# A two-layer decoder block on one core: squares on ScalarE, first units in pairs, norms read one unit later, another order in the layer opening

## The chip, the core and the metric

The kernel runs on one core of a Trainium2 chip. The metric is the device time of one launch in microseconds (us). The five engines are TensorE (PE in the rows, PEld is its weight load), VectorE (DVE), ScalarE (ACT), GpSimd (POOL) and SyncE (SP), which here only issues loads. Each runs its own instruction stream in order and waits on semaphores. A "q" behind a name (SPq, ACTq) is the engine's sequencer, which issues its DMAs.

## The reference, cut to what matters

```python
for l in range(2):
    z = rms_norm(x, mix_norm[l]) @ w_in[l]                 # x: 512 tokens x 1024
    c_q, c_kv, k_r, hq, hf, hi, hg, guv, gates = split(z)
    y_a = mla(...) @ w_branch_a[l]                         # latent attention, 8 heads
    y_b = hgrn2(hq, hf, hi, hg, lower_bounds[l], ...) @ w_branch_b[l]
    y_c = gmlp(guv, gm_ln_g[l], gm_ln_b[l], gm_w_s[l], gm_b_s[l]) @ w_branch_c[l]
    x = x + (g_a * y_a + g_b * y_b + g_c * y_c) @ w_mix_out[l]
    x = x + cross_attn(rms_norm(x, xa_norm[l]), rms_norm(mem, mem_norm[l]), ...)
    gt, up = split(rms_norm(x, ffn_norm[l]) @ ffn_w_in[l])
    x = x + (silu(gt) * up) @ ffn_w_out[l]
return rms_norm(x, final_norm)
```

gmlp takes gelu of u and v, a layer norm of v, a matmul over tokens and u times the result. hgrn2 is a gated linear recurrence in 4 heads; before its products it needs the logarithm of a forget gate made from hf.

## The kernel before, in words

x is kept transposed in SBUF: `xT` has 8 k-tiles of 128 features by 512 tokens. Matmuls run in a split form: each operand is a high part (rounded to fp32r) and a low part (the rest), and one k-tile of a product is three matmuls (high x high, high x low, low x high). hH and hL are the two parts of x times the norm's gain. The rms factor is not in them; it is applied when a product leaves PSUM, by a multiplication with `rh` on VectorE (line 1301).

The work is cut into **units**, one per 128 output columns: 24 matmuls over 8 k-tiles for those from h. A unit's weights go through three engines: SyncE loads them into one of 3 `raw` slots, ScalarE copies them to the high part in one of 4 `wH` slots (`split`, line 936), GpSimd subtracts for the low part (line 513, called a product of GpSimd below: 128x1024). A raw slot is free when GpSimd is done with it, a wH slot when TensorE has finished the unit four places earlier. The first loads of a layer wait for a count of GpSimd that also counts what GpSimd does before the layers.

`plan()` writes the order by hand: units (`u("gv", 0)`) and other steps between them. TensorE walks PLAN. ScalarE and VectorE walk READERS_PLAN, which differs in that ("norm", "mix") and ("norm", "ffn") stand one entry earlier. A step means something on each engine. The steps that matter below:

- `("norm", which)`: TensorE multiplies `sqs`, the sum of squares of x, with ones (line 660), ScalarE takes the root into rh (947), VectorE its reciprocal (1348). No unit from h can leave PSUM before.
- `gv`, `gu`: the two halves of the gMLP; scaled by rh, then gelu on ScalarE (975). `gm_sum`, `gm_mean`, `gm_var`: the layer norm of gv: gm_mean's matmul, centring, squares on ScalarE (1075), their sum on VectorE (1433), gm_var's matmul (674), root (1079), reciprocal (1437), scaling and gain (1440, 1443). `gm_vt` transposes gv on TensorE and ScalarE copies it to gvt (1083); `gm_mix` multiplies (688) and VectorE works on the result (1450, 1454, 1306).
- `lb`: some 25 tiny VectorE operations with three visits to ScalarE, for the lower bounds of the forget gate. `f_1`, `f_2`, `f_3` make the gate's logarithm. `angle` steps are four VectorE operations each on 32x512 for the rotary angles (angle_op).
- `hg_lf`: transposes the logarithm; ScalarE and VectorE split it (1097, 1306). `hg_exp` is the first product of the recurrence (713).
- `xk`, `xv`, `xq`, `x_s`: keys, values, queries and scores of the cross attention. `mix`, `xo`, `fo` end in the residual: VectorE adds to xT (1284), ScalarE makes hH and the square (902, 906), VectorE makes hL and adds the square to sqs (1264, 1274).

Before the layers, TensorE transposes x, ScalarE copies each k-tile from PSUM to xT (912) and makes hH, GpSimd squares (503), and VectorE makes hL and adds the square. k-tile 7 is left to the start of the loop over layers, where ScalarE makes four splits and then its hH and square. 7 PSUM banks are handed out in turn; the 8th is kept for long sums.

## Time and profile before

| | |
|---|---|
| time, median of 3 runs | 2306.24 us (2301.65 to 2307.18) |
| span of the profiled execution, first to last instruction | 2302.0 us |
| TensorE busy | 2206.0 us (96%) |
| VectorE, ScalarE, GpSimd busy | 54%, 43%, 39% |
| mean granted clock of TensorE | 0.990 of full |

Of the profiled execution only the span is recorded; it is 4.2 us below the median of the runs and inside their spread. In the rows a timeline line is: start in us, duration in us, engine, line of the kernel, operation, output<-inputs, count, and in brackets the engine's idle time before it and who ended it. A line of waits is: engine, waiting line <- awaited line: us in total, times, longest. Granted clock 1.00 is TensorE's 2.4 GHz, 0.50 its 1.2 GHz.

### The profile page before, as it was taken

The page shows a single profiled execution, that of the slowest core. Times are in us where ns is not written, and L with a number is a line of the kernel's source. Part 1 is how long each engine was busy: PE and PEld are TensorE (multiplying, and loading weights), DVE is VectorE, ACT ScalarE, POOL GpSimd, SP SyncE. Part 2 cuts the span into 40 slices and gives each one's busy share as a digit, 9 for nine tenths or more (in the row PEclk, how much of TensorE's full clock was granted, in tenths as well). Part 3 has the DMA queues.
Part 4 walks back from the last instruction along what each step waited for, and adds up shares of the span by engine and source line. Part 5 has one row for each costly group of instructions (what it writes and reads, how often), then busy time and mean ns, then how long its engine had stood idle before and what let it go on. Part 6 is the DMA issues. An engine that isn't in the chain of part 4 may idle for free.

```text
span 2302.0 us, 31660 instructions
## 1 busy us (share of the span) xinstructions
PE 2206.0 (96%) x10429; PEld 1788.9 (78%) x10429; DVE 1252.5 (54%) x1695; ACT 1001.0 (43%) x1455; POOL 899.5 (39%) x418
## 2 busy tenths in 40 slices
PE   6999999999999999999999999999999999999998
PEld 5787777667877888888878877776687878888886
DVE  6757666665654544441267566765556446444312
ACT  5665545444444333232356655454453444332223
POOL 4332333234544344444443332222354434444442
PEclk8999999999999999999999999999999999999999
DMA  5222221223333333333342222122343323333331
GB/s 160 72 67 65 65 57 47 56 77 112 113 95 101 90 92 101 92 98 92 95 121 65 69 60 65 39 62 52 102 115 92 109 84 95 98 101 92 94 100 63
DMA packets 368096, 197.10 MB, mean 86 GB/s; under 512 B 24268, under 2 KB 361528, under 8 KB 367928
## 3 DMA queue, kind: packets, MB, share of 16 engines
q1 hardware_dynamic: 362008, 185.68, 28.9%
q10 hardware_dynamic: 5920, 9.31, 1.3%
q8 instruction: 90, 1.47, 0.3%
q14 instruction: 78, 0.64, 0.1%
HBM read 191.68 MB, written 2.10 MB: 84 GB/s over the span
## 4 chain that ended last, share of the span: by engine, by line
PE 80%; DVE 10%; issue 5%; ACT 3%; DMA 1%; ACTq 0%; DVEq 0%; POOL 0%; SPq 0%; POOLq 0%
PE PS L573 23%; PE PS L575 23%; PE PS L574 23%; PE PS L792 2%; PE PS L733 1%; PE PS L815 1%; DVE rstd L1532 1%; DVE xqL L1306 1%; DVE mp L1612 1%; DMA spare<-mq 1%; DVE dec L1496 1%; DVE sqs L1274 1%; PE PS L630 1%; PE PS L632 1%; PE PS L631 1%
## 5 line engine op out<-in xcount | busy, mean ns | idle before, releaser
L513 POOL TENSOR_TENSOR wL<-raw,wH 128x1024 fp32r<-128x1024 f32 (+4 forms) x406 | 890.3, 2195 | 1361.0 <-ACT wH L936 1360.5
L936 ACT ACTIVATE wH<-raw 128x1024 fp32r<-128x1024 f32 (+4 forms) x406 | 384.1, 947 | 982.2 <-PE PS L575 892.1
L573 PE MATMUL PS<-hH,wH 128*128 128x512 f32 x1696 | 675.2, 398 | 16.0 <-ACT wH L936 11.0
L575 PE MATMUL PS<-hH,wL 128*128 128x512 f32 x1696 | 663.0, 391 | 0.0
L574 PE MATMUL PS<-hL,wH 128*128 128x512 f32 x1696 | 663.0, 391 | 0.0
L573 PEld LDWEIGHTS PS<-hH,wH 128*128 128x128 f32 x1696 | 319.9, 189 | 87.7 <-issue 13.1
L574 PEld LDWEIGHTS PS<-hL,wH 128*128 128x128 f32 x1696 | 320.1, 189 | 68.3 <-issue 3.6
L575 PEld LDWEIGHTS PS<-hH,wL 128*128 128x128 f32 x1696 | 319.5, 188 | 68.3
L1284 DVE TENSOR_TENSOR xT<-xT,PS 128x512 f32<-128x512 f32 x48 | 33.0, 688 | 264.3 <-PE PS L575 264.3
L1301 DVE TENSOR_TENSOR fm<-PS,rh 128x512 f32<-128x512 f32 x44 | 30.4, 692 | 201.1 <-PE PS L575 201.1
L575 PE MATMUL PS<-fH,wL 128*128 128x512 f32 x352 | 136.9, 389 | 0.0
L573 PE MATMUL PS<-fH,wH 128*128 128x512 f32 x352 | 136.9, 389 | 0.0
L574 PE MATMUL PS<-fL,wH 128*128 128x512 f32 x352 | 136.9, 389 | 0.0
L1301 DVE TENSOR_TENSOR gate<-PS,rh 128x512 f32<-128x512 f32 x92 | 63.6, 692 | 116.6 <-PE PS L575 115.8
L1306 DVE TENSOR_TENSOR fL<-fm,fH 128x512 fp32r<-128x512 f32 x44 | 122.5, 2788 | 0.0
L1274 DVE TENSOR_TENSOR sqs<-sqs,sq 128x512 f32<-128x512 f32 x48 | 110.3, 2298 | 1.0
L575 PEld LDWEIGHTS PS<-fH,wL 128*128 128x128 f32 x352 | 66.1, 188 | 13.8
L574 PEld LDWEIGHTS PS<-fL,wH 128*128 128x128 f32 x352 | 66.1, 188 | 13.7
L573 PEld LDWEIGHTS PS<-fH,wH 128*128 128x128 f32 x352 | 66.1, 188 | 13.6
L733 PE MATMUL PS<-dec 128*128 128x128 f32 x384 | 48.7, 276 | 10.0 <-DVE qcum L1498 10.0
L1512 DVE TENSOR_REDUCE attn<-mprod 128x128 f32<-128x896 f32 x32 | 56.6, 1770 | 1.1
L792 PE MATMUL PS<-mk,mq 96*128 96x128 f32 (+3 forms) x128 | 48.2, 499 | 9.3 <-DVE mq L1569 7.6
(340 smaller groups left out, 3427.9 us busy)
## 6 DMA issues: line engine op xcount, KB each, us to landing
raw<-in_w_in SPq DMA_DIRECT2D x106, 512.0 KB, 3.9
raw<-in_ffn_w_in SPq DMA_DIRECT2D x88, 512.0 KB, 3.8
raw<-in_xa_w_kv SPq DMA_DIRECT2D x32, 512.0 KB, 3.8
raw<-in_ffn_w_out SPq DMA_DIRECT2D x32, 512.0 KB, 3.9
raw<-in_w_mix_out SPq DMA_DIRECT2D x16, 512.0 KB, 4.0
raw<-in_xa_w_q SPq DMA_DIRECT2D x16, 512.0 KB, 3.9
raw<-in_xa_w_o SPq DMA_DIRECT2D x16, 512.0 KB, 4.0
raw<-in_ffn_w_out SPq DMA_DIRECT2D x16, 384.0 KB, 3.4
```

Source lines behind the costliest of these rows:

```text
L513: nc.gpsimd.tensor_tensor(wL[:, s, 0:w], raw[:, r, 0:w], wH[:, s, 0:w].bitcast(F32), ALU.subtract).then_inc(*did("gpsimd", "lo", n))
L573: nc.tensor.matmul(o, w0, xh(k0 + k), start=(first and k == 0), stop=False)
L574: nc.tensor.matmul(o, w0, xl(k0 + k), start=False, stop=False)
L575: ins = nc.tensor.matmul(o, w1, xh(k0 + k), start=False, stop=(last and k == kts - 1))
L733: ins = nc.tensor.matmul(r, dec[:, i, n, :], dec[:, i, n, :], start=True, stop=True)
L792: nc.tensor.matmul(o[:, 0:n], mq[0:96, h % 2, i * P:n], mk[0:96, h % 2, 0:n], start=True, stop=False)
L936: nc.scalar.activation(wH[:, PLACE[n] % NS, 0:w], raw[:, PLACE[n] % NR, 0:w], ACT.Copy).then_inc(*did("scalar", "hi", n))
L1274: V.tensor_tensor(sqs[:], sqs[:], sq[:, j % 2, :], ALU.add).then_inc(*(did("vector", "sqs", which) if last else did("vector", "sqs", which ...
L1284: V.tensor_tensor(xT[:, j, :], xT[:, j, :], bank(*step) if name != "fo" else bank("fo", j), ALU.add)\
L1301: V.tensor_tensor(dst, src, scale, ALU.mult).then_inc(*did("vector", *me))
L1306: V.tensor_tensor(dst, src, hi.bitcast(F32), ALU.subtract).then_inc(*did("vector", *step))
L1512: V.tensor_reduce(attn[:, i, :], mprod[:].rearrange("p n t -> p t n"), AX.X, ALU.add)\
```

## The change

1. Before the layers VectorE copies x from PSUM and ScalarE squares; GpSimd does nothing but its one memset. Each k-tile has a PSUM bank of its own, so no transpose waits for a bank.
2. `twins`: units gv 0 and gv 1, and fg 0 and fu 0, are multiplied by turns, two k-tiles of the one and then the same two of the other, so that each new k-tile of h feeds 6 matmuls instead of 3. TensorE waits for the low weights of both first.
3. The norm's matmul stands behind the pair (mix, ffn) and behind xq 0 (xa). READERS_PLAN moves the norm ahead of these units again for ScalarE and VectorE.
4. At the start of a layer ScalarE makes two splits, then hH and the square of k-tile 7, then the other two.
5. The steps of the opening stand in another order: lb from behind gv 1 to behind hf, gm_var one unit later, gm_vt behind hq 0, gm_mix behind hg 0, the angle steps shifted.

```diff
-    p = [u("gv", 0), ("norm", "mix"), ("angle", 0), u("gv", 1), ("lb",), u("gv", 2), ("angle", 1), u("gv", 3), u("hf", 0), ("gm_sum",), ("gm_ws",)]
-    p += [u("gu", 0), ("gm_mean",), u("gu", 1), ("gm_var",), ("f_1", 0), u("gu", 2), ("f_2", 0), ("angle", 2), u("gu", 3), ("angle", 3)]
-    p += [u("hi", 0), ("f_3", 0), ("gm_vt",), ("angle", 4), u("hq", 0), ("sin",), ("gm_mix",), u("hg", 0), ("hg_vt", 0)]
+    p = [u("gv", 0), u("gv", 1), ("norm", "mix"), u("gv", 2), u("gv", 3), ("angle", 0), u("hf", 0), ("gm_sum",), ("gm_ws",), ("lb",)]
+    p += [u("gu", 0), ("gm_mean",), u("gu", 1), ("angle", 1), u("gu", 2), ("gm_var",), ("f_1", 0), u("gu", 3), ("f_2", 0), ("angle", 2)]
+    p += [u("hi", 0), ("f_3", 0), ("angle", 3), u("hq", 0), ("gm_vt",), ("angle", 4), u("hg", 0), ("sin",), ("gm_mix",), ("hg_vt", 0)]
...
-    p += [u("xk", 2), u("xk", 3), ("norm", "xa"), u("xq", 0), u("xq", 1), u("xq", 2), ("x_s", 0), u("xq", 3), u("xk", 4)]
+    p += [u("xk", 2), u("xk", 3), u("xq", 0), ("norm", "xa"), u("xq", 1), u("xq", 2), ("x_s", 0), u("xq", 3), u("xk", 4)]
...
-for _s in (("norm", "mix"), ("norm", "ffn")):
-    _i = READERS_PLAN.index(_s)
-    READERS_PLAN[_i - 1:_i + 1] = [_s, READERS_PLAN[_i - 1]]
+for _s, _n in (("mix", 2), ("xa", 1), ("ffn", 2)):
+    _i = READERS_PLAN.index(("norm", _s))
+    READERS_PLAN[_i - _n:_i + 1] = [("norm", _s)] + READERS_PLAN[_i - _n:_i]
+
+TWINS = {("gv", 0): ("gv", 1), ("fg", 0): ("fu", 0)}
...
+            def twins(l, one, other):
+                us = [(u, PLACE[UNIT_AT[u]] % NS, take(l, ("u", *u), ("sc", *u))) for u in (one, other)]
+                for u in (one, other):
+                    pe.wait_ge(*after(l, "lo", UNIT_AT[u]))
+                for k0 in range(0, KT, 2):
+                    for n, (u, s, o) in enumerate(us):
+                        for k in (k0, k0 + 1):
...
-                nc.gpsimd.tensor_tensor(sqs[:] if kt == 0 else sq[:, kt % 2, :], xT[:, kt, :], xT[:, kt, :], ALU.mult)\
-                    .then_inc(*did("gpsimd", "sq", "start", kt))
...
-            for kt in range(KT):
-                act.wait_ge(*after(None, "x_t", kt))
-                nc.scalar.activation(xT[:, kt, :], bank("x_t", kt), ACT.Copy).then_inc(*did("scalar", "x0", kt))
...
+            for kt in range(KT - 1):
+                act.wait_ge(*after(None, "x0", kt))
                 high(None, "start", kt, vecs[:, VROW["mix_norm"] + kt:VROW["mix_norm"] + kt + 1])
+                if kt >= 3:
+                    act.wait_ge(*after(None, "sqs", "start", kt - 2))
+                square_of(None, "start", kt)
...
-                for n in range(NS):
+                for n in range(2):
                     split(l, n)
                 act.wait_ge(*earlier(l, "vector"))
                 high(l, "mix_last", KT - 1, col("mix_norm", KT - 1))
                 square_of(l, "mix_last", KT - 1)
+                for n in range(2, NS):
+                    split(l, n)
...
-            for kt in range(KT - 1):
-                low_x(None, "mix", kt, "start", vecs[:, VROW["mix_norm"] + kt:VROW["mix_norm"] + kt + 1])
-                add_square(None, "start", kt, "start")
+            for kt in range(KT + 1):
+                if kt < KT:
+                    dve.wait_ge(*after(None, "x_t", kt))
+                    V.tensor_copy(xT[:, kt, :], bank("x_t", kt)).then_inc(*did("vector", "x0", kt))
+                k = kt - 1
+                if 0 <= k < KT - 1:
+                    low_x(None, "mix", k, "start", vecs[:, VROW["mix_norm"] + k:VROW["mix_norm"] + k + 1])
+                    add_square(None, "start", k, "start")
```

Three places in the order of instructions. The first is ScalarE from the constants' loads on: the first splits of the layer (wH<-raw), and hH and the square of k-tile 7. Before:

```order
L922 DMA negB<-in_consts 128x64
...
L936 ACT_TABLE_LOAD
L936 ACTIVATE wH<-raw 128x1024
...
L936 ACTIVATE wH<-raw 128x1024
L953 ISA
L902 ACTIVATE hH<-xT,cur 128x512
L906 ACTIVATE sq<-xT 128x512
```

And now:

```order
L918 ACTIVATE sq<-xT 128x512
L931 DMA tri<-in_consts 128x128
...
L945 ACT_TABLE_LOAD
L945 ACTIVATE wH<-raw 128x1024
...
L945 ACTIVATE wH<-raw 128x1024
L962 ISA
L914 ACTIVATE hH<-xT,cur 128x512
L918 ACTIVATE sq<-xT 128x512
L938 ISA
```

The constants' loads and all splits now stand behind the last of seven squares, where a copy of k-tile 7 stood; behind hH and the square of k-tile 7 follow two more splits.

The second is VectorE from the last sum of squares (gsum) to the reciprocal of gm_var (rstd). gu<-PS,rh is a unit's scaling; turns and red are the angles. Before:

```order
L1433 TENSOR_TENSOR gsum<-gsum,sq 128x512
L1636 REGISTER_ALU
L1301 TENSOR_TENSOR gu<-PS,rh 128x512
L1436 REGISTER_ALU
L1437 RECIPROCAL rstd<-rstd 128x512
```

And now:

```order
L1449 TENSOR_TENSOR gsum<-gsum,sq 128x512
...
L1317 TENSOR_TENSOR gu<-PS,rh 128x512
...
L1341 TENSOR_SCALAR turns<-turns 32x512
...
L1343 SCALAR_TENSOR_TENSOR red_147<-turns,ang 32x512
...
L1343 SCALAR_TENSOR_TENSOR red_147<-turns,red_147 32x512
...
L1317 TENSOR_TENSOR gu<-PS,rh 128x512
...
L1453 RECIPROCAL rstd<-rstd 128x512
```

Four angle operations (the third line of them stands twice) and one more scaling stand between the sum and the reciprocal.

The third is ScalarE from the end of f_2 (t_98) to the copies of the transposed gv (gvt). Before:

```order
L1067 ACTIVATE t_98<-t_97 128x512
...
L936 ACTIVATE wH<-raw 128x1024
L973 REGISTER_ALU
L975 ACT_TABLE_LOAD
L975 ACTIVATE gu<-gu 128x512
...
L1083 ACTIVATE gvt<-PS 128x512
```

And now:

```order
L1078 ACTIVATE t_98<-t_97 128x512
...
L945 ACTIVATE wH<-raw 128x1024
...
L945 ACTIVATE wH<-raw 128x512
L988 REGISTER_ALU
L990 ACT_TABLE_LOAD
L990 ACTIVATE hq<-hq 128x512
L1093 REGISTER_ALU
L1094 ACTIVATE gvt<-PS 128x512
```

The silu of hq now stands ahead of the gvt copies, and two splits follow each other.

## Rows read from the trace of the kernel before

**Rows 1.** The page, part 1: busy time, share, instructions of each engine.

```profile
PE 2206.0 (96%) x10429; PEld 1788.9 (78%) x10429; DVE 1252.5 (54%) x1695; ACT 1001.0 (43%) x1455; POOL 899.5 (39%) x418
```

**Rows 2.** Waits of TensorE, whole span.

```profile
PE PS L660 <- DVE sqs L1274: 8.2, 2, 4.1
PE PS L674 <- DVE gsum L1433: 5.3, 2, 2.6
PE PS L573 <- DVE hL L1264: 1.4, 4, 0.6
```

**Rows 3.** Timeline, 0 to 34 us, all engines.

```profile
10.96 0.60 ACT L912 ACTIVATE xT<-PS 128x512 f32<-128x512 f32 x1 [1.50 <-PE PS L545]
...
16.55 0.35 ACTq L922 DMA_DIRECT2D tri<-in_consts  x1
...
18.46 0.45 ACTq L922 DMA_DIRECT2D negB<-in_consts  x1
...
20.61 1.28 ACT L936 ACT_TABLE_LOAD   x1 [2.87 <-DMA raw<-in_w_in]
...
23.05 2.34 POOL L513 TENSOR_TENSOR wL<-raw,wH 128x1024 fp32r<-128x1024 f32 x1 [2.60 <-ACT wH L936]
...
25.62 0.79 PE L573 MATMUL PS<-hH,wH 128*128 128x512 f32 x1 [10.96 <-ACT wH L936]
```

**Rows 4.** Waits of SyncE's DMA queue, 0 to 80 us.

```profile
SPq L481 <- POOL sq L503: 16.8, 3, 13.9
```

**Rows 5.** Two stretches: length, busy (count) by engine, TensorE's clock, DMA share, GB/s.

```profile
25.00:30.00 5.00, 4.38 (x10) 3.46 (x11) 0.00 (x0) 1.99 (x3) 4.83 (x3) 0.50 0.55 130
642.00:644.00 2.00, 2.00 (x6) 1.61 (x5) 1.14 (x1) 0.60 (x1) 0.00 (x0) 0.51 0.75 257
```

**Rows 6.** Three VectorE lines by themselves: duration in ns min/median/max, starts, forms.

```profile
L1274 DVE TENSOR_TENSOR sqs<-sqs,sq x48: 677/2770/2894, 10.4 to 2289.3; 128x512 f32<-128x512 f32 x48
L1264 DVE SCALAR_TENSOR_TENSOR hL<-xT,vecs,hH x7: 739/740/1021, 8.2 to 20.9; 128x512 fp32r<-128x512 f32 x7
L1620 DVE COPY mpt<-PS x32: 273/410/558, 387.9 to 1651.3; 128x384 f32<-128x384 f32 x16, 128x128 f32<-128x128 f32 x16
```

**Rows 7.** Timeline, 34 to 117 us, layer 0's opening from the norm to hg_exp.

```profile
34.50 1.02 PE L660 MATMUL PS<-sqs,ones 128*128 128x512 f32 x2
...
55.72 3.48 DVE L1327 SCALAR_TENSOR_TENSOR red<-turns,red 32x512 f32<-32x512 f32 x2
...
72.23 2.08 PE L674 MATMUL PS<-gsum,ones 128*128 128x512 f32 x2 [2.62 <-DVE gsum L1433]
...
75.38 3.35 DVE L1437 RECIPROCAL rstd<-rstd 128x512 f32<-128x512 f32 x1 [2.61 <-ACT rstd L1079]
...
81.30 3.99 DVE L1443 TENSOR_SCALAR gv<-gv,cur 128x512 f32<-128x512 f32 x4
...
94.69 2.61 DVE L1330 TENSOR_SCALAR red<-red 32x512 f32<-32x512 f32 x1
...
97.33 2.04 ACT L1083 ACTIVATE gvt<-PS 128x512 f32<-128x512 f32 x4
...
111.77 0.69 DVE L1306 TENSOR_TENSOR lfL<-PS,lfH 128x512 fp32r<-128x512 f32 x1 [1.68 <-ACT lfH L1097]
...
113.67 0.39 PE L713 MATMUL PS<-segM,lfH 128*128 128x512 f32 x1
```

**Rows 8.** Timeline of TensorE, layer 0, norm xa, first matmuls of xq 1 and xq 2.

```profile
641.05 1.14 PE L660 MATMUL PS<-sqs,ones 128*128 128x512 f32 x2 [4.11 <-DVE sqs L1274]
...
649.12 0.39 PE L573 MATMUL PS<-hH,wH 128*128 128x512 f32 x1
...
654.55 0.39 PE L573 MATMUL PS<-hH,wH 128*128 128x512 f32 x1
```

**Rows 9.** Timeline of TensorE, layer 1: the norm and hg_exp.

```profile
1164.57 1.02 PE L660 MATMUL PS<-sqs,ones 128*128 128x512 f32 x2
...
1243.61 0.39 PE L713 MATMUL PS<-segM,lfH 128*128 128x512 f32 x1
```

More of the change, by code:

```diff
@@ L138, in plan @@
     for j in range(FT):
-        p += [u("fg", j)] + ([("norm", "ffn")] if j == 0 else []) + [u("fu", j)]
+        p += [u("fg", j), u("fu", j)] + ([("norm", "ffn")] if j == 0 else [])
     p += [u("fo", j) for j in range(24)]
@@ L497, in _ @@
             nc.gpsimd.memset(ones[:], 1.0).then_inc(*did("gpsimd", "ones"))
-            for kt in range(KT - 1):
-                pool.wait_ge(*after(None, "x0", kt))
-                if kt >= 3:
-                    pool.wait_ge(*after(None, "sqs", "start", kt - 2))
-                nc.gpsimd.tensor_tensor(sqs[:] if kt == 0 else sq[:, kt % 2, :], xT[:, kt, :], xT[:, kt, :], ALU.mult)\
-                    .then_inc(*did("gpsimd", "sq", "start", kt))
             layers("gpsimd")
@@ L540, in _ @@
             for kt in range(KT):
-                b = take(None, ("x_t", kt), ("x0", kt))
+                b = PS[:, kt, :]
+                counted["bank"][("x_t", kt)] = kt
                 if kt % 2 == 0:
                     pe.wait_ge(sem(f"x_in{kt // 2}"), 16)
+                if kt == KT - 1:
+                    pe.wait_ge(*after(None, "vecs"))
                 for i in range(TT):
@@ L547, in _ @@
                 if kt == 0:
-                    b = take(None, ("vecs_t",), ("vecs",))
+                    counted["bank"][("vecs_t",)] = KT - 1
                     pe.wait_ge(sem("vectors_in"), 16)
-                    nc.tensor.transpose(b[:, 0:VROWS], rows[0:VROWS, :], ident[0:VROWS, 0:VROWS]).then_inc(*did("tensor", "vecs_t"))
-            pe.wait_ge(*after(None, "x0", KT - 1))
-            pe.wait_ge(*after(None, "vecs"))
+                    nc.tensor.transpose(PS[:, KT - 1, 0:VROWS], rows[0:VROWS, :], ident[0:VROWS, 0:VROWS]).then_inc(*did("tensor", "vecs_t"))
             layers("tensor")
-            def unit(l, name, j):
+            def twins(l, one, other):
[5 more added lines that the diff above has]
+                        for k in (k0, k0 + 1):
+                            if n == 0:
+                                pe.wait_ge(*((sem("mix_h_ready"), l * KT + (k + 1)) if u[0] == "gv" else after(l, "h_lo", "ffn", k)))
+                            w0, w1 = wH[:, s, k * P:(k + 1) * P], wL[:, s, k * P:(k + 1) * P]
+                            nc.tensor.matmul(o, w0, hH[:, k, :], start=(k == 0), stop=False)
+                            nc.tensor.matmul(o, w0, hL[:, k, :], start=False, stop=False)
+                            ins = nc.tensor.matmul(o, w1, hH[:, k, :], start=False, stop=(k == KT - 1))
+                        if k == KT - 1:
+                            ins.then_inc(*did("tensor", "u", *u))
+            def unit(l, name, j):
+                if (name, j) in TWINS.values():
+                    return
+                if (name, j) in TWINS:
+                    twins(l, (name, j), TWINS[(name, j)])
+                    return
                 n = UNIT_AT[(name, j)]
@@ L565, in product @@
                     for k in range(kts):
-                        if name == "gv" and j == 0:
-                            pe.wait_ge(sem("mix_h_ready"), l * KT + (k + 1))
-                        elif key:
+                        if key:
                             pe.wait_ge(*after(l, *key(k)))
@@ L584, in unit @@
                         key = lambda k: ("h_lo", "xa", k)
-                    if name == "fg" and j == 0:
-                        key = lambda k: ("h_lo", "ffn", k)
                     o = take(l, me, ("sc", name, j))[0:m, :]
@@ L1275, in add_square @@
                     *(did("vector", "sqs", which) if last else did("vector", "sqs", which, j)))
-            for kt in range(KT - 1):
-                low_x(None, "mix", kt, "start", vecs[:, VROW["mix_norm"] + kt:VROW["mix_norm"] + kt + 1])
-                add_square(None, "start", kt, "start")
+            for kt in range(KT + 1):
[6 more added lines that the diff above has]
+                    add_square(None, "start", k, "start")
             layers("vector")
```

5 lines of the change are left out of this document (removed).

## The prediction

> **What bounds the kernel now.** I read the page first: TensorE is busy for 2206.0 of 2302.0 us [rows 1], so only its idle time and its slow stretches can be won, and any delay that reaches it is lost in full. Then its waits: among them are two of 4.1 us for the sum of squares at norm xa, two of about 2.6 us for the sum at gm_var, and 1.4 us in all where a unit waits for the low part of k-tile 7 [rows 2]. Then the opening, where TensorE starts its first unit only at 25.62 [rows 3]. Last the granted clock: after the idle stretch at the start, and again after the 4.11 us at norm xa, TensorE runs at 0.50, which is 1.2 GHz [rows 5].
>
> **Part 1, norm xa.** Behind xq 0 the norm's matmul finds sqs ready, since xq 0 takes 654.55 − 649.12 = 5.43 us [rows 8], more than the 4.11 us. Its own k-tile 7 of h is ready in time, because it comes to that only after seven eighths of its length and the low part is made before the last addition to sqs, which takes 2.77 us [rows 6]. With the wait goes its slow stretch: from the norm to xq 1 are 649.12 − 641.05 = 8.07 us, where a unit and the norm (1.02 by the norms of rows 7 and 9) would take 6.45, so 1.6 were lost to the clock. Gain 4.11 + 1.6 = 5.7 us a layer, 11.4 in all. What is late next: rh comes some 1.5 us later on the clock but one unit nearer to the scores x_s 0, which have two units instead of three behind the norm, 10.9 us. The chain to them is root, reciprocal 3.35, two scalings of 0.7, and a high and a low part, about 9 to 10 us with one stall. I take it as covered by about 1 us.
>
> **Part 2, the pairs.** They can win the waits for k-tile 7: of the 1.4 us in four places the longest is 0.6 [rows 2]; I give 0.6 to layer 1, 0.5 to layer 0 and the rest, 0.3, to the two ffn pairs. The low weights of the second unit are ready long before in the ffn pair and in layer 1, so the pairs cost nothing there.
>
> **Part 3, the very start.** The loads of the first weights wait for squares of GpSimd now [rows 4], and this wait goes: the tiles will lie there early. But what comes next is late. VectorE now does three operations per k-tile: the copy from PSUM, which I put at 0.70 us by the two sizes of L1620 (0.56 for 384 columns, 0.27 for 128), the low part 0.74, the addition 0.68 (its shortest) [rows 6], together 2.1. k-tile 2 is in PSUM at 10.96 [rows 3]; four k-tiles later, k-tile 6 is in xT at 10.96 + 4 × 2.1 + 0.7 = 20.1. ScalarE's last hH and square wait for that, and its issue of the five constants' loads stands behind them: 18.46 + 0.45 − 16.55 = 2.4 us [rows 3], till 22.5. Only then the table load, 1.28, and the first splits. From the table load to GpSimd's product are 2.44 us (20.61 to 23.05) [rows 3]: 24.9. The pair waits for two products, 2 × 2.34: 29.6, and TensorE starts 0.23 after a product: 29.9, or 30.1 with a piece of VectorE's work between them. That is 4.5 us later than 25.62. The loads that come early hide nothing, since the splits aren't waiting for them any more.
>
> The norm's matmul of layer 0 then comes at 30.1 + (34.50 − 25.62 − 0.5) + 5.43 = 43.9 against 34.50: 9.4 later. In layer 1 it comes 5.43 − 0.6 = 4.8 later [rows 2, 9]. Whether this costs anything depends on what follows it.
>
> **Part 4, the opening of a layer.** From the norm to the first product of the recurrence TensorE needs, in both layers, 113.67 − 34.50 = 79.2 and 1243.61 − 1164.57 = 79.0 us [rows 7, 9]. In this stretch VectorE and ScalarE are nearly as full as TensorE: the last operation that the product waits for ends at 111.77 + 0.69 = 112.46, only 1.2 us ahead of it [rows 7]. So a norm that comes later pushes the whole chain, and the unit multiplied ahead of it isn't won. I walked through VectorE's, ScalarE's and GpSimd's new orders with the durations of the rows.
>
> Up to gm_var nothing changes in length: now 72.23 − 34.50 = 37.7; with lb behind hf, lb has to wait for ScalarE's five operations and table loads on hf, and the angles moved out pay for it. TensorE has done gu 2 by then, but its wait at gm_var stays near 2.5 us, and the clock falls there as now (72.23 is a 2.08 us row, where the norm's is 1.02).
>
> Behind gm_var it gets longer. Between the last sum and the reciprocal there now stand, on VectorE, four angle operations (0.4, 0.7, 0.7, 0.7) and a scaling, and then gelu, table load and root on ScalarE. A product of GpSimd runs at the first of them and the next product follows. An operation of 32 partitions stalls as long as a big one: two took 3.48 where 1.4 is their work [rows 7], one took 2.61 instead of 0.42 (94.69), and an addition takes 2.77 instead of 0.68 [rows 6]. So each stall costs 2.1. The reciprocal, now 3.15 behind the matmul (75.38 − 72.23), will be 3.2 later without a stall and 7.4 with two. Less: the scaling of gu 2 is only moved (0.7), the stall of L1443 (3.99 for four) goes as no split falls there, 2.0, and so does that of 94.69, 2.2. More: f_2 on ScalarE, four operations of about 0.65 and two table loads of 1.28, 5.2 us, now starts only behind gu 3's gelu, and VectorE has some 2.5 us of work to cover it: 2.7. The third angle step meets two products, a long one and one of half the width, 3.0, and the work on gm_mix one more, 1.7. The idle 1.7 before lfL [rows 7] and the 1.2 of slack are used up. Sum with all these stalls: 7.4 − 0.7 − 2.0 − 2.2 + 2.7 + 3.0 + 1.7 − 2.9 = 7.0. Without the stalls (4.2, 3.0 and 1.7) it is −1.9. I take 6 us per layer by which the chain from the norm to hg_exp grows: near the stalled end, since nearly every VectorE operation of the kind that meets a product in the rows pays for it in full (the median of L1274 is 2.77), and a little less, since not each meeting need come about. TensorE shows this as a wait at the first product of gm_mix: the gvt copies, now at 97.33, stand behind hq's silu, and that behind the angles.
>
> The Trainium skill, page "SBUF — State Buffer", section "SBUF: two separate sides", says that VectorE and GpSimd share one pair of ports by an exclusive lock, that the one that starts first keeps it for its whole instruction, and that only VectorE's operations in a 2-port mode or with two SBUF inputs need it. By that rule each angle operation can wait out a whole product; with a pair shared by bandwidth they would only stretch by some tenths, and the end without stalls would hold. The rows above side with the lock. What the page leaves open is who gets the pair between two products in a row, and no row shows it.
>
> **The sum.** Layer 0: 9.4 + 6 = 15.4. Layer 1: 4.8 + 6 = 10.8. Norm xa −11.4, ffn pairs −0.3. Together +14.5 on the profiled span of 2302.0: 2316.5. The median of the runs is 4.2 above that span, so 2320.7.
>
> **Rivals.**
> A. The chain has room: the new order takes as much out of it as it puts in, and only the late norms remain, less the 1.2 of slack each: 9.4 + 4.8 − 2.4 − 11.7 = about 0, so 2306. For it speaks that ScalarE and VectorE have idle time in the stretch, 2.6 us at the reciprocal and 1.7 before lfL [rows 7]. Against it speaks that these are waits of one on the other in one chain.
> B. The opening is won, too: the splits are not held, TensorE starts near 23 as the loads come early, gm_var's wait goes in both layers (2.62, and 1.0 by which its matmul runs longer than the norm's), and the norm's delay is hidden: −2.6 − 7.2 − 11.7 = −21.5, 2285; with half of the first two 2290. It needs hf, lb, mean and squares to end one unit earlier against the norm than in my walk. This is the faster side; it decides at gm_var, where the sum would have to be ready within 35 us of the norm's matmul instead of 37.7.
> C. More is lost: the wait at gm_mix lets the clock fall, gm_mix's small products and part of the unit behind them run at 0.50, and this adds 2.5 us a layer; or x_s 0 waits for xq's low part and gives back part of the 5.7: 2326 to 2330.
>
> **How the numbers follow.** Forecast 0.60, A 0.15, B 0.13, C 0.12. The forecast's own range is ±6. About 0.3% (6.9 us) is what a measurement of this kernel can tell from no change: faster means below 2299.3, slower above 2313.2. Faster has most of B and a little of A, 0.15. Within it are most of A and the lower edge of the forecast, 0.19. Slower is the rest, 0.66. The range reaches from the near edge of A, 2298, to C, 2330.
>
> **What would show it.** In the page after: SyncE's first load ahead of 3 us; the first unit's matmul at about 30; the norm at 44; no wait for sqs at norm xa, and 5.4 us from xq 0 to the norm. At gm_var a wait of 2 to 3 us, at about 37 behind the norm; at the first gm_mix product a wait for ScalarE's gvt of 6 to 10 us; hg_exp 84 to 86 behind the norm. I am wrong if TensorE starts ahead of 27, if the gm_var wait is gone, or if gm_mix starts without a wait.

## The result and the profile after

The changed kernel takes 2332.4 us (median of 4 runs, 2329.83 to 2334.07); the kernel before took 2306.7 beside it. The ratio is 1.0113, 95% interval 1.0098 to 1.0127: 1.1% slower. The forecast was 2320.7 with a range to 2330. The direction was right, the time lies outside the range. The profiled span is 2330.3 us, 28.3 more than the 2302.0 before; the medians differ by 25.7, since the profiled execution before lay 4.2 us below its median and this one 2.1.

Part 1 of the page, which answers to [rows 1]: TensorE is busy for 4.6 us more; the other 23.7 of the 28.3 us are idle time.

```profile
PE 2210.6 (95%) x10429; PEld 1793.9 (77%) x10429; DVE 1266.6 (54%) x1703; ACT 993.2 (43%) x1450; POOL 889.4 (38%) x411
```

The waits of TensorE over the whole span, which answer to [rows 2] (waiting line <- awaited, us in total, times, longest):

```profile
PE PS L700 <- ACT gvt L1094: 16.7, 2, 8.3
PE PS L563 <- POOL wL L508: 14.9, 1, 14.9
...
PE PS L587 <- DVE gate L1317: 9.6, 2, 4.8
...
PE PS L686 <- DVE gsum L1449: 4.9, 2, 2.4
```

The two waits for sqs are gone. New are 8.3 us twice at gm_mix (L700), which the prediction named, and 4.8 us twice in an ordinary unit, fg 1, which it did not. The sum at gm_var is waited for as before.

The timeline of the start and of layer 0's opening, which answers to [rows 3, 7] (start, duration, engine, line, operation, shapes, count, idle time before):

```profile
19.15 0.69 DVE L1291 COPY xT<-PS 128x512 f32<-128x512 f32 x1
...
21.01 0.69 DVE L1291 COPY xT<-PS 128x512 f32<-128x512 f32 x1
...
22.41 1.28 ACT L945 ACT_TABLE_LOAD   x1 [1.29 <-issue]
...
24.84 10.21 POOL L508 TENSOR_TENSOR wL<-raw,wH 128x1024 fp32r<-128x1024 f32 x4 [23.89 <-ACT wH L945]
...
30.07 0.79 PE L563 MATMUL PS<-hH,wH 128*128 128x512 f32 x1 [14.90 <-POOL wL L508]
...
43.23 1.02 PE L672 MATMUL PS<-sqs,ones 128*128 128x512 f32 x2
...
80.77 1.12 PE L686 MATMUL PS<-gsum,ones 128*128 128x512 f32 x2 [2.44 <-DVE gsum L1449]
80.92 4.93 POOL L508 TENSOR_TENSOR wL<-raw,wH 128x1024 fp32r<-128x1024 f32 x2 [6.17 <-ACT wH L945]
...
81.35 2.25 DVE L1341 TENSOR_SCALAR turns<-turns 32x512 f32<-32x512 f32 x1
...
83.63 2.77 DVE L1343 SCALAR_TENSOR_TENSOR red<-turns,ang 32x512 f32<-32x512 f32 x1
...
91.16 3.35 DVE L1453 RECIPROCAL rstd<-rstd 128x512 f32<-128x512 f32 x1 [2.61 <-ACT rstd L1090]
...
107.31 0.75 DVE L1492 SCALAR_TENSOR_TENSOR hlf<-t,lbc,t 128x512 f32<-128x512 f32 x1 [2.73 <-ACT t L1078]
...
108.55 2.71 DVE L1343 SCALAR_TENSOR_TENSOR red<-turns,ang 32x512 f32<-32x512 f32 x1
...
111.30 2.35 DVE L1343 SCALAR_TENSOR_TENSOR red<-turns,red 32x512 f32<-32x512 f32 x2
...
114.40 0.63 ACT L990 ACTIVATE hq<-hq 128x512 f32<-128x512 f32 x1 [4.36 <-DVE hq L1317]
...
114.94 2.04 ACT L1094 ACTIVATE gvt<-PS 128x512 f32<-128x512 f32 x4
...
115.57 5.96 PE L700 MATMUL PS<-gwT,gvt 128*128 128x128 f32 x32 [8.34 <-ACT gvt L1094]
...
128.97 0.49 PE L725 MATMUL PS<-segM,lfH 128*128 128x512 f32 x1 [1.09 <-DVE lfL L1322]
```

k-tile 6 is in xT at 19.8 (19.15 + 0.69) and k-tile 7 at 21.7, the table load follows the constants' loads at 22.41, and the first unit waits for the second of GpSimd's four products. gm_var comes 37.5 us behind the norm, as before; the reciprocal 10.4 behind gm_var's matmul instead of 3.15; the gvt copies stand behind hq's silu. hg_exp comes 85.7 us behind the norm instead of 79.2.

The norms and the place behind norm ffn, and layer 1, which answer to [rows 8, 9]:

```profile
659.94 1.02 PE L672 MATMUL PS<-sqs,ones 128*128 128x512 f32 x2
...
819.99 1.02 PE L672 MATMUL PS<-sqs,ones 128*128 128x512 f32 x2
...
821.67 3.35 DVE L1364 RECIPROCAL rh<-rh 128x512 f32<-128x512 f32 x1 [6.82 <-ACT rh L956]
...
825.06 0.69 DVE L1317 TENSOR_TENSOR gate<-PS,rh 128x512 f32<-128x512 f32 x1
...
825.80 0.79 PE L587 MATMUL PS<-hH,wH 128*128 128x512 f32 x1 [4.80 <-DVE gate L1317]
...
1187.05 1.02 PE L672 MATMUL PS<-sqs,ones 128*128 128x512 f32 x2
...
1272.76 0.49 PE L725 MATMUL PS<-segM,lfH 128*128 128x512 f32 x1 [1.23 <-DVE lfL L1322]
...
1960.01 1.02 PE L672 MATMUL PS<-sqs,ones 128*128 128x512 f32 x2
```

Norm xa (659.94) has no wait. Behind norm ffn TensorE stands until VectorE has scaled fg 0's result (gate). In the kernel before, the same two operations of VectorE came as soon behind the norm's matmul, but a unit, fu 0, still lay between the norm and fg 1, which starts at 809.63 without a wait:

```profile
803.29 1.05 PE L660 MATMUL PS<-sqs,ones 128*128 128x512 f32 x2
...
805.01 3.35 DVE L1348 RECIPROCAL rh<-rh 128x512 f32<-128x512 f32 x1 [1.85 <-ACT rh L947]
...
808.40 0.69 DVE L1301 TENSOR_TENSOR gate<-PS,rh 128x512 f32<-128x512 f32 x1
...
809.63 0.39 PE L573 MATMUL PS<-hH,wH 128*128 128x512 f32 x1
...
1933.33 1.04 PE L660 MATMUL PS<-sqs,ones 128*128 128x512 f32 x2
```

With these rows the 28.3 us divide as follows. A unit that moved from one side of a norm to the other is taken out at 5.4 us.

| stretch | predicted | measured | from |
|---|---|---|---|
| start to hg_exp, layer 0 | +15.4 | +15.3 | 128.97 − 113.67 |
| hg_exp to norm ffn, both layers (norm xa) | −11.4 | −11.9 | 691.02 − 689.62 − 5.4, and 687.25 − 689.72 − 5.4 |
| norm ffn to the end of the layer, both | −0.3 | +12.8 | 367.06 − 361.28, and 370.29 + 5.4 − 368.67 |
| norm to hg_exp, layer 1, and gv 1 ahead of it | +10.8 | +12.1 | 85.7 − 79.0 + 5.4 |
| sum | +14.5 | +28.3 | |

In the second row layer 0 has −4.0 and layer 1 −7.9. Around norm xa itself both win the same: from the first matmul of xk 2 to that of x_s 0 are 23.0 us instead of 29.0. The rest are stretches at half clock that moved (last section), and between the two layers they cancel.

### The profile page after: what moved, and what is told of

Its sections match the earlier page's. It is cut to its first block, busy times and chain, and to the rows that moved or that the text cites. A ratio compares the mean times of both kernels' runs of the same rounds, so it can differ in the third digit from the quotient of the medians.

```text
span 2330.3 us, 31649 instructions
## 1 busy us (share of the span) xinstructions
PE 2210.6 (95%) x10429; PEld 1793.9 (77%) x10429; DVE 1266.6 (54%) x1703; ACT 993.2 (43%) x1450; POOL 889.4 (38%) x411
## 4 chain that ended last, share of the span: by engine, by line
PE 79%; DVE 10%; issue 6%; ACT 3%; DMA 1%; ACTq 0%; DVEq 0%; POOL 0%; POOLq 0%
PE PS L587 22%; PE PS L589 22%; PE PS L588 22%; PE PS L804 2%; PE PS L745 1%; PE PS L827 1%; DVE rstd L1548 1%; PE PS L563 1%; PE PS L564 1%; PE PS L565 1%; DVE red L1343 1%; DVE mp L1628 1%; DVE dec L1512 1%; DMA spare<-mq 1%; PE PS L643 1%
## 5 line engine op out<-in xcount | busy, mean ns | idle before, releaser
L587 PE MATMUL PS<-hH,wH 128*128 128x512 f32 x1632 | 648.4, 397 | 14.6 <-DVE gate L1317 9.6
L589 PE MATMUL PS<-hH,wL 128*128 128x512 f32 x1632 | 638.7, 391 | 0.0
L588 PE MATMUL PS<-hL,wH 128*128 128x512 f32 x1632 | 638.2, 391 | 0.0
L587 PEld LDWEIGHTS PS<-hH,wH 128*128 128x128 f32 x1632 | 308.1, 189 | 82.7 <-DVE gate L1317 11.3
L588 PEld LDWEIGHTS PS<-hL,wH 128*128 128x128 f32 x1632 | 308.3, 189 | 65.2 <-issue 2.4
L589 PEld LDWEIGHTS PS<-hH,wL 128*128 128x128 f32 x1632 | 307.6, 188 | 65.6
L588 PEld LDWEIGHTS PS<-fL,wH 128*128 128x128 f32 x352 | 66.1, 188 | 13.8
```

The source lines that it names most:

```text
L587: nc.tensor.matmul(o, w0, xh(k0 + k), start=(first and k == 0), stop=False)
L588: nc.tensor.matmul(o, w0, xl(k0 + k), start=False, stop=False)
L589: ins = nc.tensor.matmul(o, w1, xh(k0 + k), start=False, stop=(last and k == kts - 1))
```

## The experiments

Times are medians; the ratio is to the kernel before, run beside them, with its 95% interval. Letter a: built from the changed kernel, b: from the kernel before, c: a combination. Other lines are as in the kernel that the name points to. The changed kernel was not measured again beside these runs, in which the kernel before had medians from 2303.9 to 2305.2 against 2306.7; so a difference to its 2332.4 is good to some 3 us, and the distances inside a profile carry the argument.

**a_pad.** The skip of banks moves from norm ffn to fg 5.

```diff
-                        if which == "ffn":
-                            turn[0] += known.get("pad", 0)
...
+                        if step == ("u", "fg", 5):
+                            turn[0] += known.get("pad", 0)
```

> The changed kernel, with the skip of PSUM banks that stands at norm ffn moved to unit fg 5. Theory T1 (the bank): fg 1 takes the bank of fg 0 because of the skip, and must wait until fg 0 is scaled, behind the late norm; moved away, the two waits of 4.8 us at fg 1 go and with them about 1.7 us of low clock each: 13 us less than the changed kernel, about 2319. Rival T2 (the pair and the late norm themselves hold fg 1 up, whichever bank it has): the wait of 4.8 stays or moves to fu 1, time unchanged, 2332.

Measured: 2317.2 us, ratio 1.0054 (1.0037 to 1.0071): 15.2 less than the changed kernel. The 17 us behind norm ffn (length, then TensorE, weight load, VectorE, ScalarE, GpSimd busy, clock, DMA share, GB/s), first the changed kernel, then a_pad:

```profile
821.01:838.01 17.00, 12.21 (x45) 9.95 (x46) 6.12 (x5) 6.51 (x8) 7.11 (x3) 0.80 0.21 63
```

```profile
815.78:832.78 17.00, 17.00 (x77) 14.03 (x76) 10.81 (x9) 8.70 (x11) 9.79 (x4) 1.00 0.36 105
```

T1 holds and T2 falls: pair and late norm are the same, the wait is gone, and with it the slow clock behind it. From norm ffn to layer 1's norm a_pad takes 1175.17 − 814.76 = 360.4 us, the changed kernel 367.1 and the kernel before 361.3; from norm ffn of layer 1 to the end it takes 363.2, which is the 368.7 of the kernel before less fu 0's 5.4.

**a_oldorder.** The opening's steps in the order of before, except for the pair and its norm (the plan in short).

```diff
-[gv 0, gv 1, norm, gv 2, gv 3, angle 0, hf, gm_sum, gm_ws, lb, gu 0, gm_mean, gu 1, angle 1, gu 2, gm_var, f_1, gu 3, f_2, angle 2, hi 0, f_3, angle 3, hq 0, gm_vt, angle 4, hg 0, sin, gm_mix]
+[gv 0, gv 1, norm, angle 0, lb, gv 2, angle 1, gv 3, hf, gm_sum, gm_ws, gu 0, gm_mean, gu 1, gm_var, f_1, gu 2, f_2, angle 2, gu 3, angle 3, hi 0, f_3, gm_vt, angle 4, hq 0, sin, gm_mix, hg 0]
```

> The changed kernel with the steps of the opening in the order of before, but for the pair and its norm. Theory O (the new order makes the chain longer): from the norm to hg_exp 79 us as before instead of 85.7, the wait at gm_mix gone, gm_var's wait near 2.6; 6.7 less in each layer and 2319 in all. Rival P (the norm that comes later makes the chain longer in any order, since units run on while nothing is scaled): norm to hg_exp stays at 84 to 86 and the time within 4 of 2332.

Measured: 2322.5 us, ratio 1.0081 (1.0064 to 1.0097), 9.9 less; norm to hg_exp 79.4 us in layer 0 and 79.6 in layer 1. O holds for the length. But TensorE now waits 4.7 us at gm_mean and 1.5 to 1.9 at gm_var: the unit that was multiplied ahead of the norm is paid back there.

**Single steps of the order.** Each of these puts one or two steps of the changed order back. a_angle: angle 1 behind gm_var. a_vt: gm_vt ahead of hq 0. a_ang_early: angle 1 behind angle 0.

```diff
a_angle
-gu 1, angle 1, gu 2, gm_var
+gu 1, gu 2, gm_var, angle 1
a_vt
-hq 0, gm_vt
+gm_vt, hq 0
a_ang_early
-angle 0, hf, ..., gu 1, angle 1, gu 2
+angle 0, angle 1, hf, ..., gu 1, gu 2
```

> The changed kernel with the second angle step behind gm_var instead of ahead of gu 2. Theory S (its four VectorE operations stall behind GpSimd's products ahead of the reciprocal): the reciprocal comes 4 to 6 us earlier behind gm_var's matmul (10.4 now), the wait of 8.3 at gm_mix falls to about 3, and the kernel takes 7 to 10 us less, 2322 to 2325. Rival G (ScalarE is late: f_2, gu 3's gelu and hq's silu stand ahead of the gvt copies): the reciprocal moves but the gvt copies do not, the gm_mix wait stays above 7, time within 3 of 2332.

Measured: 2330.8 us, ratio 1.0113 (1.0096 to 1.0130).

> The changed kernel with gm_vt back ahead of hq 0. Theory V (ScalarE copies gvt only behind hq's silu, because gm_vt stands behind hq 0; hq's scaling stands behind the angles): gvt is copied right behind f_2 at about 108 instead of 115, the wait of 8.3 us at gm_mix falls to about 1, norm to hg_exp falls from 85.7 to about 79, and the kernel takes 12 to 14 us less than the changed one, 2318 to 2320. Rival W (VectorE's chain of angles, f_3 and scalings is as late as gvt): hg_exp stays 83 or more behind the norm, at most 5 us less in all, 2327 or above.

Measured: 2332.6 us, ratio 1.0124 (1.0107 to 1.0141).

> The changed kernel with the second angle step right behind the first, ahead of hf, as many units ahead of gm_var as before. Theory D (VectorE's queue sets the length of the opening: it was busy for 34.0 of 41.4 us between gm_var and hg_exp before the change and for 40.2 of 48.2 after it, and the second angle step with its 6.4 us is the difference): VectorE has room for it ahead of gm_var, hg_exp comes 79 to 80.5 us behind the norm instead of 85.7, and the kernel takes 10 to 13 us less, 2319 to 2322. Rival E (the step only moves the same time to the other side of gm_var): TensorE's wait at gm_var grows from 2.4 to 5 us or more, hg_exp stays 84 or more behind the norm, time within 4 of 2332.

Measured: 2332.6 us, ratio 1.0121 (1.0105 to 1.0138).

All three theories of a single cause fall. In a_angle, as its rival G said, the reciprocal does come 5.8 us earlier against gm_var's matmul, and hg_exp only 0.9 against the norm (the last row; first the reciprocal, then what VectorE did instead):

```profile
84.50 3.35 DVE L1453 RECIPROCAL rstd<-rstd 128x512 f32<-128x512 f32 x1 [3.48 <-ACT rstd L1090]
...
87.89 4.69 DVE L1456 TENSOR_TENSOR gv<-gv,rstd 128x512 f32<-128x512 f32 x4
...
94.57 0.42 DVE L1341 TENSOR_SCALAR turns<-turns 32x512 f32<-32x512 f32 x1
...
105.57 0.75 DVE L1492 SCALAR_TENSOR_TENSOR hlf<-t,lbc,t 128x512 f32<-128x512 f32 x1 [2.73 <-ACT t L1078]
...
127.22 0.49 PE L725 MATMUL PS<-segM,lfH 128*128 128x512 f32 x1 [1.01 <-DVE lfL L1322]
```

VectorE now idles for 3.5 us ahead of the reciprocal, time that the angle operations had filled; a stall of 2.2 us moved to the scaling of gv; and the angles are done behind it. In a_vt gvt is copied at 108.0 instead of 114.9 and the wait at gm_mix is gone, but TensorE waits 3.2 to 4.9 us at gm_vt and 4.3 to 5.4 at hg_exp. In a_ang_early the wait at gm_var grows from 2.4 to 6.4 us and that at gm_mix falls to 4.1, as the rival said.

**a_lb, a_lb_ang, a_gmvar.** lb behind the norm again; this with angle 1 behind angle 0; and the old order of a_oldorder with gm_var behind gu 2, f_1 and f_2 straight behind it.

```diff
a_lb
-norm, gv 2, ..., gm_ws, lb, gu 0
+norm, lb, gv 2, ..., gm_ws, gu 0
a_gmvar (against a_oldorder)
-gm_var, f_1, gu 2, f_2
+gu 2, gm_var, f_1, f_2
```

> The changed kernel with lb back behind gv 1 (the norm's readers first), all else of the new order kept. Theory L (lb behind hf is what costs: in the profiles with it there VectorE spends 12.5 us from lb's first to its last operation, 4.0 of them waiting for ScalarE, which must first do hf's exponential and logarithm with two table loads; in the old place it spends 8.7, at a time when nothing is late): the wait at gm_var goes, the second angle step is done before gm_var's matmul, hg_exp comes 79 to 81 behind the norm instead of 85.7: 9 to 12 less than 2332, 2320 to 2323. Rival M (what costs is gm_var behind gu 2): hg_exp 83.5 or more behind the norm, 2328 or above.

Measured: 2330.5 us, ratio 1.0117 (1.0093 to 1.0142). The wait at gm_var is gone, but TensorE waits 4.3 us at gm_mean and 6.4 at gm_mix, and hg_exp is not earlier.

> As a_lb, and the second angle step ahead of hf. By theory L everything early then stands where it stood before, but for gm_var behind gu 2: equal to a_lb within 2. If lb and the angle step must both be back: a_lb near 2328, this one near 2320. By M both stay at 2328 or above.

Measured: 2339.2 us, ratio 1.0141 (1.0122 to 1.0160), the slowest of all; TensorE waits 6.9 us at gm_mean and 5.8 at gm_mix.

> The changed kernel in the old order of steps (2322.5 as measured), but with gm_var behind gu 2 for all engines, as in the change. Theory L: the wait at gm_var (1.5 and 1.9) goes, but its matmul comes 5.4 us less these later, and VectorE does gu 2's scaling first: 0 to 3 us a layer more, 2322 to 2328. Rival M: it carries the whole loss of the new order, 2330 or above.

Measured: 2320.2 us, ratio 1.0075 (1.0059 to 1.0092), not to be told from a_oldorder. From norm to hg_exp it takes 80.4 and 80.9 us, 1.0 and 1.3 more than a_oldorder. Neither L nor M holds: lb's place isn't the cause (a_lb), and gm_var one unit later, together with the earlier f_2, costs 1.0 to 1.3 us a layer in the old order and not 6.

**a_tail.** What the six slow orders share is the tail: angle 3 behind f_3, ahead of hq's scaling. Here angle 3 goes ahead of hi 0 and gm_vt ahead of hq 0.

```diff
-f_2, angle 2, hi 0, f_3, angle 3, hq 0, gm_vt, angle 4
+f_2, angle 2, angle 3, hi 0, f_3, gm_vt, hq 0, angle 4
```

> The changed kernel with angle 3 ahead of hi 0 and gm_vt ahead of hq 0, both together, as before the change. Theory T (the tail: with angle 3 behind f_3, VectorE idles 2.7 us for f_2 and then does angle 3, 5.5 us with its stalls, ahead of hq's scaling, silu and the gvt copies): angle 3 fills the idle time, gvt is copied at about 108 and hq scaled at 108, hg_exp comes 78.5 to 80.5 behind the norm instead of 85.7, and the kernel takes 10 to 13 us less than 2332: 2319 to 2322. Rival S (the 6 us are the sum over the whole stretch, and what is taken out of one place turns up in the next, as with the other single steps): 83 or more behind the norm, 2328 or above.

Measured: 2323.9 us, ratio 1.0088 (1.0072 to 1.0103), 8.5 less than the changed kernel. VectorE's hlf, hq's scaling and hg_exp in it:

```profile
106.72 0.75 DVE L1492 SCALAR_TENSOR_TENSOR hlf<-t,lbc,t 128x512 f32<-128x512 f32 x1 [0.33 <-ACT t L1078]
...
107.51 0.69 DVE L1317 TENSOR_TENSOR hq<-PS,rh 128x512 f32<-128x512 f32 x1
...
107.54 2.04 ACT L1094 ACTIVATE gvt<-PS 128x512 f32<-128x512 f32 x4
...
124.67 0.49 PE L725 MATMUL PS<-segM,lfH 128*128 128x512 f32 x1 [2.33 <-DVE lfL L1322]
```

The idle 2.7 us ahead of hlf are 0.3, the copies of gvt and the scaling of hq start at 107.5, and hg_exp comes 82.0 us behind the norm (82.1 in layer 1). T is right as to where the larger part sits, 3.7 of 6.6 us, and wrong in that it expected all of it. Of the 3.7, gm_vt's place alone gives 1.4 (a_vt); angle 3 alone was not tried. The order's variants, layer 0, from the windows view between the two matmuls:

| | norm to hg_exp | VectorE busy in it | VectorE idle |
|---|---|---|---|
| before | 79.2 | 64.3 | 14.9 |
| changed | 85.7 | 68.9 | 16.8 |
| a_angle | 84.9 | 67.2 | 17.7 |
| a_vt | 84.3 | 68.6 | 15.7 |
| a_ang_early | 85.1 | 66.9 | 18.2 |
| a_lb | 85.5 | 67.4 | 18.1 |
| a_lb_ang | 88.6 | 66.3 | 22.3 |
| a_tail | 82.0 | 68.2 | 13.9 |
| a_oldorder | 79.4 | 65.2 | 14.2 |
| a_gmvar | 80.4 | 64.0 | 16.5 |

**b_xa.** The kernel before with norm xa behind xq 0.

```diff
-("norm", "xa"), u("xq", 0), u("xq", 1)
+u("xq", 0), ("norm", "xa"), u("xq", 1)
...
-for _s in (("norm", "mix"), ("norm", "ffn")):
+for _s in (("norm", "mix"), ("norm", "xa"), ("norm", "ffn")):
```

> The kernel before with only norm xa moved behind xq 0 (readers' order as in the change). By the prediction's part 1: both waits of 4.11 us go with 1.6 us of low clock each, 11.4 less than before, about 2295. Rival: the scores x_s 0 wait for xq's low part and give back half or more, 2300 or above.

Measured: 2296.3 us, ratio 0.9959 (0.9945 to 0.9973): faster by 8.6 us. Both waits are gone. The scores x_s 0 start without a wait, as before. The 11.4 came: from xk 2 to x_s 0 each layer takes 6.0 us less. The profiled span is only 7.1 shorter, since stretches at half clock lie elsewhere in this profile (last section).

**b_pair.** The kernel before with gv 0 and gv 1 as a pair and the norm behind them, in the order of a_oldorder.

```diff
-    p = [u("gv", 0), ("norm", "mix"), ("angle", 0), u("gv", 1), ("lb",),
+    p = [u("gv", 0), u("gv", 1), ("norm", "mix"), ("angle", 0), ("lb",),
```

> The kernel before with gv 0 and gv 1 as a pair and the norm behind them, all else as before (first of lb and the angles included). Theory N (the later norm pushes the whole chain, whatever unit is multiplied ahead of it): first unit at 28.5, as it waits for the low weights of both, norm 6 to 7 us later in layer 0 and 4.8 in layer 1, 79.4 from the norm to hg_exp, 9 to 11 us more than before: 2314 to 2316. Rival F (the unit multiplied ahead of the norm is won where the waits at gm_mean and gm_var take it up): 2304 to 2308.

Measured: 2317.7 us, ratio 1.0053 (1.0034 to 1.0071), 12.5 more. First unit 28.37, norm 42.07, hg_exp 79.5 behind it and 7.9 us later than before in layer 0, 15.9 in layer 1. N holds, F falls: the pair is a loss by itself.

**a_start.** The changed kernel with the part ahead of the layers, and the order of the first splits, as before.

> The changed kernel with the part ahead of the layers, and the order of the first splits, as before. By the prediction's part 3 the new start costs 4.5 us at the first unit and all of it reaches the end: 4.5 less, 2327.5. Rival: with the pair, TensorE then stands for k-tile 7 or for the second unit's low weights, and the norm comes at 43 all the same: within 1.5 of 2332. The turn of ScalarE's splits can add up to 1 us of waiting for k-tile 7 in layer 1.

Measured: 2332.4 us, ratio 1.0122 (1.0104 to 1.0140). First unit 28.45, norm 41.24: 2.0 us of the start reach the norm and hg_exp (126.99), and 1.8 are still there at hg_exp of layer 1; the 4.5 did not come, nor did the rival's norm at 43, though the time is the rival's. At the end nothing is left: from norm xa to norm ffn of layer 1 this profile takes 1.6 us more than the changed kernel's, with a stretch at half clock at 1899 that the other does not have, and from there to the end 0.6 more, which no row explains.

**a_fix.** Bank, order and start undone together.

> The changed kernel with three parts undone at once: the bank skip away from norm ffn, the opening's steps in the order of before, and the part ahead of the layers as before. What is left of the change: the two pairs and the three later norms. If the parts add up (bank -15, order -10, start -2), 2305. Rival: they overlap, since each wait that goes uncovers the next; 2312 or above.

Measured: 2305.6 us, ratio 1.0002 (0.9993 to 1.0012). The parts add up to what was expected, 2305. What is left of the change (pairs and later norms) is worth nothing that these runs can tell: 0.4 us, −1.6 to 2.8 by the interval. b_pair's 12.5 eat b_xa's 8.6 and would leave a loss of 3.9; the profiled execution of a_fix shows 3.2.

**b_loads and c_xa_early.** SyncE's first three loads wait for GpSimd's memset alone; then this with b_xa and the constants' loads ahead of ScalarE's copies.

```diff
-                        sp.wait_ge(*before(l, "lo", user(PLACE[n] - NR + NU + 1)))
...
+                        sp.wait_ge(sem("gpsimd_done"), l * max(b + k - 1, 1) + 1)
```

> The kernel before, but SyncE's first three loads do not wait for GpSimd's squares. If the loads of the first weights bind the start (ScalarE waits 2.87 us for raw ahead of its table load, [rows 3]): the table load follows the constants' loads at 18.9 and the first unit starts 1.7 us earlier, at 23.9, 2303 in all. Rival: the early weights take bandwidth from x, x arrives 1 us or more later, and the first unit does not move: 2305 or above.

Measured: 2303.75 us, ratio 0.9997 (0.9988 to 1.0007). First unit 24.39, 1.2 earlier and not 1.7; norm and hg_exp 1.3 and 1.2 earlier: plain in the profile, too small for the timed runs.

> The kernel before with norm xa behind xq 0, the free first loads, and the five constants' loads issued ahead of ScalarE's copies of x. Expected: 8.6 less by norm xa as measured, 1.7 by the loads and up to 2.4 by the constants' loads: first unit at 21.5 to 22, 2292 to 2293 in all. Rival: TensorE starts early but waits for k-tiles 6 and 7 of h, so that the norm comes no earlier: 2295 to 2297.

Measured: 2292.0 us, ratio 0.9949 (0.9933 to 0.9966). First unit 23.85, not 21.5: the first of GpSimd's products starts at 20.83, behind its last square, and takes 2.8.

**c_half, c_splits, c_f2.** On c_xa_early: gm_var's matmul between the fourth and fifth k-tile of gu 2 on TensorE alone. On c_half: two splits, k-tile 7, two splits; or f_2 straight behind f_1.

```diff
+                        if (name, j) == ("gu", 2) and k == KT // 2:
+                            ov = take(l, ("gm_var",), ("gm_std",))
+                            pe.wait_ge(*after(l, "gm_var_sum"))
+                            nc.tensor.matmul(ov, ones[:], gsum[:], start=True, stop=True).then_inc(*did("tensor", "gm_var"))
```

> The kernel with norm xa moved, free first loads and early constants (2292), and gm_var's matmul in the middle of unit gu 2 on TensorE, so that TensorE does not stand for the sum. If the chain of VectorE and ScalarE from the norm to hg_exp sets the end of the opening: it had only 1.2 us of room, the wait of 2.6 at gm_var turns into one of 1 to 2 at hg_exp, and 1 to 3 us are won in both layers together, 2289 to 2291. Rival: the wait and the slow clock behind it are won in full, 3.5 a layer, 2285.

Measured: 2287.7 us, ratio 0.9930 (0.9914 to 0.9947), the fastest kernel of the study. The wait at gm_var is gone and hg_exp comes 77.6 behind the norm instead of 79.0, in both layers: 1.45 each, 2.9 together, as the chain theory says (1 to 3). The median fell by more, 4.3, and the wait comes back at gm_mix with 2.4 us, not at hg_exp.

> The best kernel so far (2287.7) with ScalarE's order of the first splits as in the change: two splits, hH and square of k-tile 7, then the other two. In the profile with four splits first, k-tile 7 waits for the fourth split, which waits for its weights; TensorE stands 1.2 us for it in layer 0. Expected: that goes, 1 us less, 2286.7. Rival: the low weights of gv 1 are late in its place, no change.

Measured: 2292.3 us, ratio 0.9953 (0.9936 to 0.9969). The norm of layer 0 comes 1.7 earlier, but in layer 1 it waits 1.7 for sqs and the opening takes 80.0 us instead of 77.6: a miss, since only layer 0 was looked at.

> The best kernel so far (2287.7; gm_var's matmul in the middle of gu 2) with f_2 straight behind f_1. By theory T the stretch behind the reciprocal is a chain of VectorE and ScalarE in which f_2 waited behind gu 2's gelu: up to 3 us shorter, and TensorE, with 75.2 of 77.6 us busy, can win at most 2.4 a layer: 2284 to 2287. Rival: f_2 delays gu 2's gelu and a split behind it, TensorE waits for low weights, 2288 or above.

Measured: 2294.1 us, ratio 0.9962 (0.9948 to 0.9975), slower than c_half. The opening takes 0.95 us a layer more, 1.9 of the 7.9 us between the two profiles; the other 6.0 lie in later stretches whose order is the same, among them half clock at 1344 to 1351. In the opening, with f_2 ahead, ScalarE makes its splits late and in a row, so do GpSimd's products, and VectorE's operations run into them:

```profile
87.78 3.50 DVE L1334 SCALAR_TENSOR_TENSOR red<-turns,red 32x512 f32<-32x512 f32 x2
87.83 9.89 POOL L515 TENSOR_TENSOR wL<-raw,wH 128x1024 fp32r<-128x1024 f32 x4 [14.69 <-ACT wH L943]
...
93.74 2.84 DVE L1483 SCALAR_TENSOR_TENSOR hlf<-t,lbc,t 128x512 f32<-128x512 f32 x1
```

## Why the prediction was wrong, step by step

**Part 2, the pairs: the step that failed.** It said "so the pairs cost nothing there" of the ffn pair, from the low weights alone. It left out whose bank the next unit takes. TensorE hands out 7 banks in turn, and at norm ffn it skips four, so that a layer ends on the bank on which it began. With the pair fg 0 has bank 6, fu 0 bank 0, the norm bank 1, and fg 1, four banks skipped, bank 6 again. It comes free when fg 0 is scaled, and that now stands a whole unit later against TensorE, behind norm, root and reciprocal. Before, fg 0 and fg 1 shared bank 6 too, but the scaling ended at 808.40 + 0.69 = 809.1, and fg 1 began, a norm and a unit behind 803.29, at 809.6. The stretches behind norm ffn were put at −0.3 and measured +12.8, which is 13.1 of the 13.8 us by which the sum was too low; a_pad takes 15.2 off the median and brings these stretches to −0.9 and 0.0. The k-tile 7 that the pairs were to win was worth at most 0.6 a place.

**Part 1, norm xa.** Right: no wait, 11.9 us for 11.4; x_s 0's cover held, it starts without a wait. The 1.4 us that TensorE waits at x_s 1 are as before (1.37 for 1.39).

**Part 3, the start.** First unit at 30.07 for a predicted 30.1, norm at 43.23 for 43.9, with each k-tile of VectorE at 1.86 us instead of 2.1 and x itself 0.7 later. The exact first number is in part luck: k-tile 6 was 0.3 earlier than the 20.1 of the sum, for these two errors of opposite sign. What it put on the start as a whole divides in two: b_pair shows 2.8 of the 4.5 us as the pair's wait for the second unit's low weights, a_start 1.6 as the rest of the new start (VectorE's copies, the constants' loads behind them, the order of the splits). Layer 0's 15.3 for 15.4 are luck as well: the norm came 8.7 later and not 9.4, the opening grew by 6.6 and not 6.

**Part 4, the opening.** The size was right, 6.6 and 6.7 for 6 (7.0 before the discount), and so were its signs: gm_var's wait 2.4 at 37.5 behind the norm, gm_mix's 8.3, hg_exp at 85.7. Only the clock did not fall at gm_var in layer 0: its matmul takes 1.12 us there, not 2.08. The list of causes was half right. The two terms of the tail, f_2's 2.7 and angle 3's 3.0, are there (2.73 idle ahead of hlf, 2.71 and 2.35 in the angle) and a_tail gets 3.7 of them back. The largest term, 4.2 us of stalls ahead of the reciprocal, is there too (81.35, 83.63), and taking it away changes hg_exp by 0.9. So the sum came out, but its terms are not prices that can be had back one by one: when one goes, an idle time or another stall takes its place. The last 2.6 us a layer of the order are not put down to one step by any run; angle 1, lb and gm_var were tried, all three together only as part of the whole old order.

**The rivals.** A needed room in the chain behind a late norm; b_pair shows none, with 79.5 us from norm to hg_exp in the old order. B did not come; its point, the sum ready within 35 us of the norm, was missed at 37.5. C named slow stretches at gm_mix, and these are there: its matmuls take 5.96 us where they take 3.73 at full clock. They did not add to the opening: in a_vt gm_mix takes 3.73, and TensorE then waits at hg_exp, 4.3 us instead of 1.1.

**From span to median.** The sum added 4.2 us; the median lay 2.1 above the span.

## What to carry to other kernels

Before a norm or any other reader is moved behind more work, count the buffers in turn, skips included: who takes the buffer that this reader frees, and how much room there was (here 0.5 us). A chain over three engines is not mended by moving its worst stall: put the whole order back first, then halve it, and judge by the distance between two fixed matmuls. From norm to hg_exp it is the same in both layers within 0.2 us in the kernel before, in the changed one and in a_oldorder and a_tail (0.4 to 1.5 apart in a_gmvar, a_lb and a_ang_early), while the four runs of the changed kernel spread over 4.2 us. Work multiplied ahead of a norm is won only if what hangs on the norm has room; here, where it had 1.2 us, the cheapest gain was to fill the wait from inside a unit.
